# A three-block kernel: expert weights loaded at other times and into other places, and the first two experts' tokens gathered one expert at a time

## The reference, cut to what matters

```
merged = sigmoid(ga) * (u @ w_proj_a) + sigmoid(gb) * (attention @ w_proj_b)
x      = x + gate * (merged @ w_out)
aff    = softmax(modulated_rms_norm(x) @ w_router)        # 512 tokens x 16 experts
for each expert e: the 64 tokens with the largest aff[:, e]
    xe = their normalised rows                             # 64 x 1024
    y  = (silu(xe @ gate_e) * (xe @ up_e)) @ down_e        # 1024 -> 2048 -> 1024
    x[those tokens] += gate2 * aff * y
```

## Time and profile before

| | us |
|---|---|
| median of 3 runs | 3746.38 |
| lowest, highest run | 3745.59, 3747.65 |
| the profiled execution's own time | 3748.78 |
| its span | 3747.0 |

### The profile page before, as it was taken

The page is one execution under the profiler, slowest core; times in us unless marked ns, Lnnn a source line. Parts: engine busy times, 40 slices in busy tenths (PEclk is TensorE's granted clock), DMA queues, the critical chain, the costliest instruction groups (busy, mean ns, idle before and its releaser), DMA issues. The chain is left out here.

```text
span 3747.0 us, 57543 instructions
## 1 busy us (share of the span) xinstructions
PE 3460.5 (92%) x25148; PEld 2400.0 (64%) x25148; DVE 1433.5 (38%) x3009; ACT 673.4 (18%) x1483; POOL 77.9 (2%) x128
## 2 busy tenths in 40 slices
PE   8999999798898988899888899999999999999997
PEld 5877888333332333257676777878887856887666
DVE  2465455211011110134676344345523623534344
ACT  2217311100000000012342125112100001101231
POOL 0000000000000000000222000000000000000000
PEclk9999999999999999999999899999999999999999
DMA  6430121999999999930000310222222111221110
GB/s 243 157 145 14 46 90 56 395 428 428 428 427 426 423 427 427 427 138 1 4 4 4 107 35 23 79 82 90 86 72 90 68 68 68 68 90 38 50 63 23
DMA packets 125849, 593.82 MB, mean 158 GB/s; under 512 B 7296, under 2 KB 37632, under 8 KB 99232
## 3 DMA queue, kind: packets, MB, share of 16 engines
q1 hardware_dynamic: 125600, 590.14, 39.5%
HBM read 588.02 MB, written 2.10 MB: 157 GB/s over the span
## 5 line engine op out<-in xcount | busy, mean ns | idle before, releaser
L2742 PE MATMUL banks<-slabs,ring 128*128 128x256 f32 (+1 forms) x3912 | 872.9, 382 | 0.2 <-DVE ring L2893 0.2
L2742 PEld LDWEIGHTS banks<-slabs,ring 128*128 128x128 f32 x3912 | 740.6, 190 | 117.3 <-issue 10.5
L2100 PE MATMUL banks<-ring,slabs 128*64 128x512 f32 x2304 | 516.7, 596 | 84.0 <-DMA ring<-in_w_exp 72.0
L2100 PEld LDWEIGHTS banks<-ring,slabs 128*64 128x64 f32 x2304 | 162.8, 137 | 413.6 <-issue 319.5
L393 PE MATMUL banks<-slabs,ring 128*128 128x264 f32 (+3 forms) x1224 | 344.9, 439 | 6.0 <-PEq L323 2.5
L393 PEld LDWEIGHTS banks<-slabs,ring 128*128 128x128 f32 (+1 forms) x1224 | 229.7, 191 | 104.2 <-issue 67.9
L2237 DVE TENSOR_TENSOR work<-work,banks 128x512 f32<-128x512 f32 x32 | 22.0, 688 | 488.8 <-PE banks L2100 488.8
L2742 PE MATMUL banks<-ring 128*128 128x256 f32 (+1 forms) x848 | 197.6, 381 | 0.9 <-PEq L323 0.7
L2100 PE MATMUL banks<-slabs 128*64 128x512 f32 x768 | 171.9, 596 | 21.3 <-DMA slabs<-in_w_exp 18.4
L2742 PEld LDWEIGHTS banks<-ring 128*128 128x128 f32 x848 | 160.1, 190 | 26.8 <-issue 4.5
L2987 PE MATMUL banks<-slabs,ring 128*128 128x264 f32 x768 | 172.4, 386 | 1.6 <-issue 1.6
(11 more groups left out here) (566 smaller groups left out, 4058.8 us busy)
## 6 DMA issues: line engine op xcount, KB each, us to landing
ring<-in_w_exp SPq DMA_DIRECT2D x144, 2048.0 KB, 15.8
slabs<-in_w_exp SPq DMA_DIRECT2D x48, 2048.0 KB, 32.1
ring<-in_w_in SPq DMA_DIRECT2D x19, 2048.0 KB, 11.8
ring<-in_w_ff SPq DMA_DIRECT2D x16, 2048.0 KB, 8.3
ring<-in_even_w_in SPq DMA_DIRECT2D x14, 2048.0 KB, 8.0
ring<-in_w_ada SPq DMA_DIRECT2D x12, 2048.0 KB, 10.7
ring<-in_w_out SPq DMA_DIRECT2D x4, 2048.0 KB, 8.0
ring<-in_even_w_out SPq DMA_DIRECT2D x4, 2048.0 KB, 8.0
```

Source lines behind the costliest of these rows:

```text
L2100: ins = mm(out[64 * c:64 * c + CAP, :], lhsT[:, k, :], w[:, at:at + 512], start=first and k == 0, stop=last and k == 3)
L2742: last = mm(bank, a[:, k, :], b[:, k, :], start=k == 0, stop=k == h - 1)
```

## The change

It does four things.

1. The order of places: expert tiles 0 and 1 go to slabs 6 and 4, tiles 2 and 3 to slabs 5 and 1, tiles 4, 5 and 6 to ring slots 2, 0 and 1, tile 7 to ring slot 3, and so round until tile 95. From tile 96 on it is slots 0, 1, 2, 3 as before.
2. `expert_weights` on SP: once pa's last tile has been used, tiles 0 and 1; once pb's, tiles 2 to 6 (each still behind the tile that had its place); once wo's, tile 7. `weight_limit` is 29 until then. wo's sums move from slab 4 to slab 2.
3. The first pair is gathered one expert at a time: `gather_one(e)` makes all eight channel chunks for one expert's 64 columns, two chunks to each of four banks; it is called for expert 0 ahead of tile 0 and for expert 1 behind tile 3. `fetch_one` reads each bank as it is full.
4. The one-hot matrix of the first expert is written by the router's lane, ahead of the block boundary (`pick_one`), that of the second behind it.

The counts of the semaphores are shifted to fit. Blank lines are left out of the diff.

```diff
--- before.py
+++ after.py
@@ -31,7 +31,7 @@
-MORE_SLOTS, WIDE_RING = (5, 6, 4, 1), 8 * EXPERT_TILES
+MORE_SLOTS, WIDE_RING = (6, 4, 5, 1), 8 * EXPERT_TILES
...
@@ -283,11 +283,12 @@
-        slots = SLOTS + len(MORE_SLOTS)
+        slots, first = SLOTS + len(MORE_SLOTS), expert_tiles[0]
+        freed = [*range(SLOTS, slots), *((first + i) % (SLOTS - 1) for i in range(SLOTS - 1)), SLOTS - 1]
...
         for n in range(len(self.tiles)):
             at = n - expert_tiles[0]
-            slot = at % (slots if at < WIDE_RING else SLOTS) if n in expert_tiles else n if n < SLOTS else n % (SLOTS - 1)
+            slot = (freed[at % slots] if at < WIDE_RING else at % SLOTS) if n in expert_tiles else n if n < SLOTS else n % (SLOTS - 1)
...
@@ -1587,7 +1588,7 @@
-    core.weight_limit = core.expert_tile + SLOTS - 1
+    core.weight_limit = core.expert_tile
     with core.stage() as block:
...
@@ -1824,7 +1825,7 @@
-    wo = SevenProducts(core, "wo", act_of(merged), SEQ, flat[4], Carve(places[0]), to_raw, added, "dve",
+    wo = SevenProducts(core, "wo", act_of(merged), SEQ, flat[2], Carve(places[0]), to_raw, added, "dve",
...
@@ -1834,16 +1835,16 @@
-    router = Router(core, x, squares, gained, row, wo)
+    router = Router(core, x, squares, gained, row, wo, core.c("first", "iota"))
...
     def expert_weights(sp):
...
-        sp.wait_ge(core.weight_used.sem, core.done)
-        wo.pair_done(sp, 3)
-        core.weight_limit = core.expert_tile + SLOTS + len(MORE_SLOTS)
-        core.issue_weights(sp, core.done)
+        for used, tiles in ((pa, 2), (pb, 4 + SLOTS - 1), (wo, 4 + SLOTS)):
+            sp.wait_ge(core.weight_used.sem, used.last_tile + 1)
+            core.weight_limit = core.expert_tile + tiles
+            core.issue_weights(sp, core.done)
     stage.transfers = expert_weights
...
@@ -1878,7 +1879,8 @@
-    def __init__(self, core, x, squares, gained, row, outputs):
+    def __init__(self, core, x, squares, gained, row, outputs, iota):
+        self.iota = iota
...
@@ -2007,7 +2009,18 @@
-        yield
+        pick_one(core, core.area[:, 1024:1536].rearrange("p (t s) -> p t s", t=4), self.iota, self.rank, 0)
+        yield
+def by_expert(t):
+    return t.rearrange("p t (e s) -> p t e s", e=2)
+def pick_one(core, onehot, iota, rank, e):
+    return core.nc.vector.tensor_tensor(by_expert(onehot)[:, :, e, :], iota.unsqueeze(1).broadcast_to([P, 4, CAP]),
+                                        rank[:, :, e].unsqueeze(2).broadcast_to([P, 4, CAP]), ALU.is_equal)
...
 def experts(core, x, xtok, rank, aff, iota, gain, shift):
@@ -2025,6 +2038,7 @@
+    quarter = lambda ch: (XB[0], CB[0], XB[1], CB[1])[ch // 2][:, ch % 2 * P:ch % 2 * P + P]
...
@@ -2052,17 +2066,29 @@
+            def gather_one(e):
+                if e:
+                    pe.wait_ge(moe["picked"].sem, moe["picked"].at(1))
+                    pe.wait_ge(moe["xe_act"].sem, moe["xe_act"].at(1))
+                    pe.wait_ge(moe["xe_dve"].sem, moe["xe_dve"].at(1))
+                mine = slice(e * CAP, (e + 1) * CAP)
+                for ch in range(KC):
+                    for t in range(4):
+                        last = mm(quarter(ch)[:, mine], xtok[:, t, ch * P:(ch + 1) * P], onehot[:, t, mine], start=t == 0, stop=t == 3)
+                    if ch % 2:
+                        last.then_inc(moe["xe_full"].sem, moe["xe_full"].add(1))
...
                 for half in halves:
-                    if i >= 1:
-                        if half == 0:
-                            pe.wait_ge(moe["xe_act"].sem, moe["xe_act"].at(i))
-                            pe.wait_ge(moe["spread_read"].sem, moe["spread_read"].at(i))
-                        else:
-                            pe.wait_ge(moe["xe_dve"].sem, moe["xe_dve"].at(i))
+                    if half == 0:
+                        pe.wait_ge(moe["xe_act"].sem, moe["xe_act"].at(i + 1))
+                        pe.wait_ge(moe["spread_read"].sem, moe["spread_read"].at(i))
+                    else:
+                        pe.wait_ge(moe["xe_dve"].sem, moe["xe_dve"].at(i + 1))
                     for c in range(4):
...
@@ -2073,7 +2099,7 @@
             def turn_onehot(i):
...
-                pe.wait_ge(moe["xe_act"].sem, moe["xe_act"].at(i + 1))
+                pe.wait_ge(moe["xe_act"].sem, moe["xe_act"].at(i + 2))
...
@@ -2110,7 +2136,6 @@
-                        gather(0, (kh,))
...
                         fetched = (moe["xe_act"], moe["xe_dve"])[kh]
...
@@ -2135,14 +2160,17 @@
+            gather_one(0)
             for e in range(EXPERTS):
...
-                if s == 0 and i >= 1:
-                    pe.wait_ge(moe["xe_act"].sem, moe["xe_act"].at(i + 1))
-                    pe.wait_ge(moe["xe_dve"].sem, moe["xe_dve"].at(i + 1))
+                if e == 1 or s == 0 and i >= 1:
+                    pe.wait_ge(moe["xe_act"].sem, moe["xe_act"].at(i + 2))
+                    pe.wait_ge(moe["xe_dve"].sem, moe["xe_dve"].at(i + 2))
                 widen(e, 0, "gate")
                 widen(e, 0, "up")
+                if e == 0:
+                    gather_one(1)
...
                 if s == 1 and i + 1 < PAIRS:
@@ -2161,9 +2189,17 @@
+            def fetch_one(e):
+                mine = slice(e * CAP, (e + 1) * CAP)
+                for k in range(4):
+                    act.wait_ge(moe["xe_full"].sem, moe["xe_full"].at(4 * e + k // 2 + 1))
+                    ins = nc.scalar.activation(xe[0][:, k, mine], quarter(k)[:, mine], ACT.Identity, scale=gain[:, k:k + 1], bias=shift[:, k:k + 1])
+                ins.then_inc(moe["xe_act"].sem, moe["xe_act"].add(1))
             def fetch(i):
...
-                act.wait_ge(moe["xe_full"].sem, moe["xe_full"].at(2 * i + 1))
+                act.wait_ge(moe["xe_full"].sem, moe["xe_full"].at(KC + 2 * i - 1))
...
@@ -2186,11 +2222,13 @@
-            fetch(0)
+            fetch_one(0)
             for e in range(EXPERTS):
...
                 silu(e, 0)
+                if e == 0:
+                    fetch_one(1)
...
@@ -2209,21 +2247,31 @@
             def pick(i):
...
-                by_expert = lambda t: t.rearrange("p t (e s) -> p t e s", e=2)
...
-                slots = iota.unsqueeze(1).unsqueeze(1).broadcast_to([P, 4, 2, CAP])
-                nc.vector.tensor_tensor(by_expert(onehot), slots, all4(rank), ALU.is_equal).then_inc(moe["picked"].sem, moe["picked"].add(1))
+                if i == 0:
+                    pick_one(core, onehot, iota, rank, 1).then_inc(moe["picked"].sem, moe["picked"].add(1))
+                else:
+                    slots = iota.unsqueeze(1).unsqueeze(1).broadcast_to([P, 4, 2, CAP])
+                    nc.vector.tensor_tensor(by_expert(onehot), slots, all4(rank), ALU.is_equal).then_inc(moe["picked"].sem, moe["picked"].add(1))
                 dve.wait_ge(moe["picked"].sem, moe["picked"].at(2 * i + 1))
...
+            def fetch_one(e):
+                mine = slice(e * CAP, (e + 1) * CAP)
+                for k in range(4, KC):
+                    dve.wait_ge(moe["xe_full"].sem, moe["xe_full"].at(4 * e + k // 2 + 1))
+                    ins = nc.vector.tensor_scalar(xe[0][:, k, mine], quarter(k)[:, mine], gain[:, k:k + 1], shift[:, k:k + 1], ALU.mult, ALU.add)
+                ins.then_inc(moe["xe_dve"].sem, moe["xe_dve"].add(1))
             def fetch(i):
...
-                dve.wait_ge(moe["xe_full"].sem, moe["xe_full"].at(2 * i + 2))
+                dve.wait_ge(moe["xe_full"].sem, moe["xe_full"].at(KC + 2 * i))
...
@@ -2267,18 +2315,20 @@
-                dve.wait_ge(moe["xe_act"].sem, moe["xe_act"].at(PAIRS))
-                dve.wait_ge(moe["xe_dve"].sem, moe["xe_dve"].at(PAIRS))
+                dve.wait_ge(moe["xe_act"].sem, moe["xe_act"].at(PAIRS + 1))
+                dve.wait_ge(moe["xe_dve"].sem, moe["xe_dve"].at(PAIRS + 1))
...
             pick(0)
-            fetch(0)
+            fetch_one(0)
             for e in range(EXPERTS):
...
                 hidden(e, 0)
+                if e == 0:
+                    fetch_one(1)
...
```

## The result

| | before | after |
|---|---|---|
| median of 15 runs, us | 3748.45 | 3754.90 |
| ratio of the two, 95% interval | | 1.0020, 1.0012 to 1.0028 |
| the profiled execution, us | 3748.78 | 3760.93 |
| its span, us | 3747.0 | 3759.2 |

What follows compares the result with a forecast made beforehand. The experts' stage was taken as bound by its transfers. Tile 12 would begin at 714.9 us instead of 715.9, and that 1.0 us off the median of 3746.38 gave 3745.4 us, range 3741.0 to 3749.0.

Steps and rivals of the forecast that it cites:

- The early loads and places: Ahead of the experts' stage: first eight tiles in by some 664 us instead of 690, alone worth nothing.
- the rival of the stall at the change of places: At tile 96, eight places become four: costs only if PE runs over 4.5 us later; 0.05 together with a collision.
- The price of a 64-column product: In both gathers: charged the full 128-column price, 7.2 us more PE work; 0.211 us each at the low clock.
- The half-price gather: Rival at both gathers: halved columns halve the cost, a gain of 6.0 us, 3740.4 us; chance 0.07.
- The step that failed: In the first gather: clock rises at about 684.2 us, 25.6 products at the low clock, 38.4 at full.
- first gather, to tile 0's start: Expert 0's 64 products ahead of tile 0, from 678.8 to 688.5 us.
- tile 4 used: Behind the second gather: tile 4 is used at 713.2 us, which lets tile 12 be issued.
- 1.7 us of restart: After a rest of DMA: transfers run as if started at full rate 1.7 us behind the tile's issue.
- The slower rival: At tile 12's issue: the two gathers cost more than the rest they remove, up to 2.7 us; chance 0.16.
- G: The time expert 0 is gathered and tile 0 starts: 688.5 us, bounds 686.0 to 692.3; gain is 689.6 − G.
- Its other thought: In the slower rival: the moment of the clock's rise differs between runs, so a loss may show in one only.
- the dip of DMA of 1.4 us: Near 713 us, before tile 12: a rest of 1.4 us replaces the rest at 698.

Runs made afterwards that it cites:

- e1: The kernel before with only the new places, earlier loads and moved wo's sums, old gather kept; ratio to before 1.0000.
- e9: e7 with the old places, times of issue and wo's sums; ratio to the kernel before 0.9985.
- e7: The changed kernel with the pair's 128-column gather ahead of tile 0, no second gather, and 12 unused products in the router; ratio to before 0.9984.
- e2: The changed kernel with old places and times of issue: only the one-expert gather and early one-hot matrix remain; ratio to before 1.0017.
- e8: The changed kernel with expert 0's 64-column gather made twice, the first for nothing; one run, 3776.14 us.
- e5: The changed kernel with 12 unused products on PE in the router, ahead of its wait for DVE's search; ratio to before 1.0017.
- e11: e5 once more, the same program, for a second profile; one run, 3750.11 us.
- e10: e3 plus 64 products of 64 columns behind tile 3 whose result nobody reads; ratio to the kernel before 1.0002.
- e3: The changed kernel with the whole pair's 128-column gather ahead of tile 0 and no second gather; ratio to the kernel before 0.9990.
- e4: The changed kernel with 24 unused products on PE in the router, which held back its last transpose; ratio to before 1.0016.

## Why the prediction was wrong

**The bound was read rightly.** The stage is set by its transfers: the last tile waits for DMA in every profile, and what counts is when they begin to run unbroken.

**The early loads and places: right,** worth nothing that the runs could tell from zero (e1 within 3.4 us, e9 against e7), and the rival of the stall at the change of places did not come.

**The price of a 64-column product: right at both clocks.** 64 take 7.36 us at full clock (7.2 forecast) and 13.89 us at the low one, 0.217 us each (0.211 taken). The half-price gather, the rule of "throughput is purely N cycles" from the Trainium skill ("TensorE: Matmul & The Clock Gate", part 2, FILL), did not come: 64 and 128 columns both take about 7.4 us, where each product has its own 128x128 stationary operand.

**The step that failed is the clock.** The prediction said "The clock rose at about 684.2", and carried that moment over to products of another width: 25.6 of them at the low clock, 38.4 at the full one. The mechanism of the sum was right and this term of it was wrong. In the changed kernel, in e2 and in e8 no product of the first gather saw the clock rise: it rose only in the tiles behind, at 699.5, 694.9 and 711.4. Less the shift, the terms are these:

| term | forecast | measured |
|---|---|---|
| gather starts | 678.8 | 678.3 |
| first gather, to tile 0's start | 9.7 us | 13.8 us |
| tiles 0 to 3 | 13.85 us | 16.5 us |
| second gather | 7.2 us | 7.3 us |
| tile 4 used | 713.2 | 719.6 |

With the same 1.7 us of restart, tile 12 begins at 721.3 instead of 714.9, against 715.9 before: 5.4 of the 7.1 us. The other 1.7 lie in the long stretch from tile 12 to the last tile: 889.8 us against 888.1 before. e5 and e11, one program, take 889.8 and 888.0 us for it, so 1.7 us is no more than the scatter between two profiles. Whether a part of it belongs to the change is not shown.

**The slower rival named the mechanism and was given 0.16.** Its place and its deciding point (G over 689.6) were right: G came out at 692.1. Its price of up to 2.7 us was too small, because it let the low clock end with the gather. The clock came up only 5.3 us into the tiles, and that cost 2.65 us more. Its reason against, "it rose 5 us after PE began", was a reading of 128-column products. Its other thought, that the late rise may show in one run and not in the next, did not come either: the changed kernel, e2 and e8 all show it.

**The rest of the sum holds.** e10, where the clock does rise in the first gather, gave G and tile 4's use within 0.1 us of the forecast and the dip of DMA of 1.4 us. G is that close in part by luck: the gather began 0.2 us and the clock rose 0.3 us earlier than forecast, and the products took a little longer.

## What to carry to other kernels

Where a stage is bound by transfers, ask when the first buffers come free. The few microseconds of PE work ahead of the first release then cost their full length, and loading the first buffers sooner was worth nothing here, since they were all in by that release. A granted clock is no property of a moment in the program: before a piece of TensorE work is replaced at a spot where the clock is low, find a row in which products of the new shape lifted it, and without one price the work and some 3 to 5 us behind it at the low clock (3.0 us in e5, 5.3 in the changed kernel). Splitting a product along its moving side saved nothing here, since 64 and 128 moving columns cost the same with a new 128x128 stationary operand each; it cost both the time and the clock.

## What the runs showed of the hardware that I had not expected

- TensorE stayed at 1.2 GHz through 27.5 us of unbroken 64-column products with a new 128x128 stationary operand each (e8). In the same place 128-column products lifted it 5.3 us after they began (e3, e10; 5.1 before, 4.4 in e1). The Trainium skill ("TensorE: Matmul & The Clock Gate", part 1) says that idleness throttles the clock and activity releases it. These runs agree for 128 columns and for the tiles. For 64 columns they do not, if busy is what the profile calls busy: it showed PE at 100% in both cases.
- The clock even fell from 2.4 to 1.2 GHz 1.7 us into such products, without idle time among them (e5 and e11 alike), and once it did not (e4, 7.33 us). Behind tile 3 it stayed up through all of them in every profile (7.36 us). Why is open.
- 24 instructions of 512 columns took 10.46 us (0.43 us each) where the stationary operand has 128 columns. An expert tile's, with 64 and the same 512 moving columns, take 3.46/16 = 0.22 us each, also at full clock. No run varied the stationary width alone.
